# A two-block network in fp32: the mixer's products without halves, GpSimd freed in the first layer, and streamed buffers on multiples of 256

## The reference

```
h = rmsnorm(x) * (1 + scale) + shift          # channel by channel
layer 0:  u = h @ w_in                        # 1024 x 1024
          per group g of 256 channels, window w in (2, 4, 8, 16):
            pooled = trailing mean of u over w positions - u
            y_g = pooled @ w_grp[g]           # 256 x 256
          y = (concat(y_g) * scale) @ w_out   # 1024 x 1024
layer 1:  y = dilated attention (three branches, 16 heads each) @ w_o
x = x + gate * y
x = x + gate2 * ((silu(conv3(a)) * v) @ w_down), [a, v] = h @ w_up   # 2816 wide
```

## Time and profile before

| | |
|---|---|
| median of 3 runs | 2838.7 us (2837.08 to 2839.62) |
| the profiled execution | 2840.38 us, span 2838.6 us |
| TensorE busy | 2723.9 us, 96% of the span |
| VectorE busy | 1523.9 us, 54% |
| ScalarE busy | 1062.1 us, 37% |
| GpSimd busy | 388.6 us, 14%, nearly all in the first fifth |
| moved by DMA | 297.19 MB, 105 GB/s on average |
| chain that ended last | 89% TensorE, 3% VectorE, 1% ScalarE |

### The profile page before, as it was taken

How to read it: one execution, slowest core, us unless ns; L and a number is a source line. 1 busy time by engine, 2 the same in 40 slices (tenths; PEclk the granted TensorE clock), 3 DMA queues, 4 the chain that set the end, 5 groups by cost and what they waited for, 6 DMA issues and landing times.

```text
span 2838.6 us, 30758 instructions
## 1 busy us (share of the span) xinstructions
PE 2723.9 (96%) x12742; PEld 2186.1 (77%) x12742; DVE 1523.9 (54%) x2035; ACT 1062.1 (37%) x1488; POOL 388.6 (14%) x196
## 2 busy tenths in 40 slices
PE   5689999989999999899999999999999999999998
PEld 3568888778888887688888777788887777788886
DVE  7888857655555555654345555443344455443343
ACT  3333233344444444343234455422223455422231
POOL 3444545410000000000000001010010011010010
PEclk9799999999999999999999999999999999999999
DMA  7354645321212111122222221222223212223222
GB/s 271 119 210 183 248 177 198 135 83 60 75 61 74 69 66 60 60 89 101 95 89 102 97 75 60 76 102 97 89 95 113 90 60 75 76 103 101 85 100 71
DMA packets 45690, 297.19 MB, mean 105 GB/s; under 512 B 4976, under 2 KB 5104, under 8 KB 16368
## 3 DMA queue, kind: packets, MB, share of 16 engines
q1 hardware_dynamic: 45408, 294.71, 28.6%
q10 hardware_dynamic: 144, 0.52, 0.1%
HBM read 293.12 MB, written 2.10 MB: 104 GB/s over the span
## 4 chain that ended last, share of the span: by engine, by line
PE 89%; DVE 3%; ACT 1%; issue 1%; POOL 0%; DVEq 0%; ACTq 0%; POOLq 0%
PE PS L433 87%; PE PS L478 2%; DVE XT L1237 0%; DVE H2Lb L1234 0%; DVE WL L1234 0%; ACT H1H L821 0%; DVE AA L1234 0%; DVE H1L L1234 0%; DVE AR L1256 0%; ACT WH L821 0%; DVE T0c L1234 0%; DVE T1a L1234 0%; DVE T1c L1234 0%; ACT AA L821 0%; DVE T0a L1234 0%
## 5 line engine op out<-in xcount | busy, mean ns | idle before, releaser
L433 PE MATMUL PS<-H1H,WH 128*128 128x512 f32 x2240 | 898.2, 401 | 39.0 <-DVE H1L L1234 32.5
L433 PE MATMUL PS<-H1H,WL 128*128 128x512 f32 x2240 | 878.6, 392 | 0.0
L433 PE MATMUL PS<-H1L,WH 128*128 128x512 f32 x2240 | 877.8, 392 | 0.0
L1234 DVE TENSOR_TENSOR WL<-RAW,WH 128x1024 fp32r<-128x1024 f32 (+1 forms) x330 | 435.2, 1320 | 381.4 <-ACT WH L821 380.5
L821 ACT ACTIVATE WH<-RAW 128x1024 fp32r<-128x1024 f32 (+2 forms) x409 | 449.9, 1102 | 268.5 <-PE PS L433 257.7
L433 PEld LDWEIGHTS PS<-H1H,WH 128*128 128x128 f32 x2240 | 424.2, 189 | 143.6 <-issue 44.7
L433 PEld LDWEIGHTS PS<-H1L,WH 128*128 128x128 f32 x2240 | 424.8, 190 | 90.5 <-issue 5.3
L433 PEld LDWEIGHTS PS<-H1H,WL 128*128 128x128 f32 x2240 | 423.9, 189 | 91.0
L1687 POOL TENSOR_TENSOR WL<-RAW,WH 128x1024 fp32r<-128x1024 f32 (+2 forms) x79 | 229.8, 2914 | 235.8 <-ACT WH L821 235.6
L1256 DVE CUSTOM_DVE_ANT_0 AR<-AR,COND,CO 128x1024 f32<-128x1024 f32 x112 | 237.3, 2161 | 0.4
L433 PE MATMUL PS<-H2Hb,WH 128*128 128x512 f32 x384 | 160.0, 417 | 11.5 <-DVE H2Lb L1234 11.5
(11 more groups left out here) (246 smaller groups left out, 3334.3 us busy)
## 6 DMA issues: line engine op xcount, KB each, us to landing
RAW<-stream SPq DMA_DIRECT2D x170, 1024.0 KB, 4.8
AR<-stream SPq DMA_DIRECT2D x56, 1024.0 KB, 6.9
RAW<-stream SPq DMA_DIRECT2D x64, 704.0 KB, 4.0
RT<-ret SPq DMA_DIRECT2D x2, 1536.0 KB, 6.3
RAW<-stream SPq DMA_DIRECT2D x4, 640.0 KB, 6.9
XT<-xt SPq DMA_DIRECT2D x2, 1024.0 KB, 8.9
y<-XT SPq DMA_DIRECT2D x8, 256.0 KB, 2.5
ATT<-att SPq DMA_DIRECT2D x1, 576.0 KB, 3.4
```

Of the source, the lines that this page charges most:

```text
L433: return nc.tensor.matmul(out, weights, moving, start=start, stop=stop, skip_group_check=True)
L1234: return nc.vector.tensor_tensor(out, a, b, op)
```

## The change

- **Mixer without halves.** The input products (64 of them: 8 output chunks by 8 blocks) and the group products (16) are single fp32 matmuls on the raw weights and on an unsplit activation: HF takes the place of H1H and H1L for the input, PM that of H2Ha and H2La. ScalarE and GpSimd no longer make halves of tiles 0 to 8 or of the pooled chunks; VectorE writes the pooled chunk straight to PM. The first four weight units get buffers of their own (MIX0 to MIX3, over WH and WL).
- **Groups one by one.** The group products run group by group, both output halves in turn, and `w_out` takes its input chunks in the order in which they are made.
- **GpSimd idle ahead of the attention.** VectorE makes all low halves of weights from tile 9 on and all low halves in the norms.
- **Modulation.** The gates are computed between the last input chunks and behind the group products, the other units of the mixer between out products by explicit calls; AR has five slots for the first 16 units, then three. SP issues six units ahead of the small table `BAS`, in place of four.
- **Addresses.** Every streamed activation and weight buffer starts on a multiple of 256 bytes; the others are moved to make room.

```diff
-        units += [shift[i], scale[i], ("main", None, [("pool_w_in", 0, 2 * i, 2, 8 - GRP, GRP)])]
-    side = ada("ada_w", 0, 16, list(range(16, 48)))
+        units += [scale[i], shift[i], ("mix", None, [("pool_w_in", 0, 2 * i, 2, 8 - GRP, GRP)])]
+    gate = ada("ada_w", 0, 16, list(range(16, 24)))
...
-    units += pool[:1]
-    out, side = mix(pool[1:], side, 2)
+    units += pool[:1] + gate[:2] + pool[1:2] + gate[2:]
+    out, side = mix(pool[2:], ada("ada_w", 0, 24, list(range(24, 40))), 2)
...
-BYDVE = 79
+SLOTS = [n % 5 if n < 16 else n % 3 for n in range(sum(1 for u in UNITS if u[0] == "ada"))]
+SPLIT = 9
...
-        self.H1H, self.H1L = at("H1H", 17536, 4096, F32R), at("H1L", 33920, 4096, F32R)
+        self.H1H, self.H1L = at("H1H", 18432, 4096, F32R), at("H1L", 35072, 4096, F32R)
-        self.WH = [at(f"WH{i}", 66688 + 5632 * i, WSLOT, F32R) for i in range(3)]
-        self.WL = [at(f"WL{i}", 83584 + 5632 * i, WSLOT, F32R) for i in range(3)]
+        self.WH = [at(f"WH{i}", 68096 + 5632 * i, WSLOT, F32R) for i in range(3)]
+        self.WL = [at(f"WL{i}", 84992 + 5632 * i, WSLOT, F32R) for i in range(3)]
+        self.MIX = [at(f"MIX{i}", a, 1280) for i, a in enumerate((68096, 73728, 79360, 84992))]
+        self.PM, self.HF = at("PM", 159744, 4096), at("HF", 18432, 4096)
-        self.AH, self.AL = at("H2Hb", 109632, 4096, F32R), at("H2Lb", 126016, 4096, F32R)
+        self.AH, self.AL = at("H2Hb", 110592, 4096, F32R), at("H2Lb", 127488, 4096, F32R)
-        self.GH = [at("GHa", 158784, 5632, F32R), at("GHb", 130112, 5632, F32R)]
-        self.GL = [at("GLa", 181312, 5632, F32R), at("GLb", 152640, 5632, F32R)]
+        self.GH = [at("GHa", 160768, 5632, F32R), at("GHb", 131328, 5632, F32R)]
+        self.GL = [at("GLa", 183808, 5632, F32R), at("GLb", 153856, 5632, F32R)]
-        gh, gl = at("GHd", 113728, 5632, F32R), at("GLd", 136256, 5632, F32R)
+        gh, gl = at("GHd", 114688, 5632, F32R), at("GLd", 139264, 5632, F32R)
-        self.HH, self.HL = at("H2Hc", 113728, 4096, F32R), at("H2Lc", 130112, 4096, F32R)
+        self.HH, self.HL = at("H2Hc", 115456, 4096, F32R), at("H2Lc", 132096, 4096, F32R)
...
+    def plain(t, H, ready, freed):
+
+        b = BANK[t]
+        w, sem, value = c.whole(t)
+        q.wait_ge(sem, value)
+        vacate(b)
+        for k in range(8):
+            q.wait_ge(*ready(k))
+            ins = mm(PS[b][:, :], w[:, 128 * k:128 * k + 128], chunk(H, k), k == 0, k == 7)
+        ins.then_inc(c.mm, 1)
+        free[b] = freed
...
-                ins = three(x, t, 128 * (GRP * j + x), chunk(c.H1H, k), chunk(c.H1L, k), k == 0, k == 7)
+                o = 128 * (GRP * j + x)
+                ins = mm(PS[x][:, :], w[:, o:o + 128], chunk(c.HF, k), k == 0, k == 7)
...
-    for d in range(2):
-        t = 7 + d
-        q.wait_ge(*c.low(t))
-        for e, g in enumerate(GROUPS):
+    for e, g in enumerate(GROUPS):
+        for d in range(2):
...
-                q.wait_ge(c.pl, POOLED.index(n) + 1)
-                ins = three(b, t, 128 * n, chunk(c.PH, n), chunk(c.PL, n), i == 0, i == 1)
+                q.wait_ge(c.p3, POOLED.index(n) + 1)
+                ins = mm(PS[b][:, :], w[:, 128 * n:128 * n + 128], chunk(c.PM, n), i == 0, i == 1)
...
+    for i in range(8):
+        pooled(i)
+    prep(9)
+    for e, g in enumerate(GROUPS):
+        for d in range(2):
             n = 2 * g + d
...
+    prep(10)
+    modulation()
+    modulation()
     for n in range(8):
         prep(11 + n)
+        q.wait_ge(c.ada, 12)
         residual(RES["pool"], n, 9 + n, 16)
         add_square(1, n)
+        modulation()
```

More of the change, by code:

```diff
@@ L285, in __init__ @@
[L285 to L294, removed]
@@ L389, in low, with whole, slot @@
     def low(self, t):
-        return (self.lop, t + 1) if t < BYDVE else (self.lod, t + 1 - BYDVE)
+        return self.lod, t + 1 - SPLIT
+    def whole(self, t):
+        u, j = TILES[t]
+        n = PLACE[u]
+        if UNITS[u][0] == "mix":
+            return self.MIX[n], self.mix[n], 16
+        o = sum(words(x) for x in UNITS[u][2][:j])
+        return self.RAW[n % 2][:, o:o + words(UNITS[u][2][j])], self.raw[n % 2], 16 * (n // 2 + 1)
+    def slot(self, u):
+        n = PLACE[u]
+        i = SLOTS[n]
+        return self.AR[i], self.ara[i], 16 * SLOTS[:n + 1].count(i)
     def narrow(self, u, hh):
@@ L513, in pe_program @@
     for n in range(3):
-        gemm(4 + n, c.H1H, c.H1L, h, (c.pu, POOLED.index(n) + 1))
-    for d in range(2):
-        t = 7 + d
-        q.wait_ge(*c.low(t))
-        for e, g in enumerate(GROUPS):
+        plain(4 + n, c.HF, mixed_in, (c.pu, POOLED.index(n) + 1))
+    for e, g in enumerate(GROUPS):
+        for d in range(2):
             b = BANK["grp", d, g]
+            w, sem, value = c.whole(7 + d)
+            q.wait_ge(sem, value)
             vacate(b)
@@ L884, in act_program @@
         high(0, 0, 2 * i + 1, 0, 0)
-    prep(5)
-    def pooled(i):
-        n = POOLED[i]
+    for i, n in enumerate(POOLED):
         b = n - 3 if i < 5 else BANK[4 + n]
@@ L1230, in dve_program @@
     PS = c.PS
-    made, unit, adas, steps = 0, 0, 0, 0
+    made, adas, steps = SPLIT, 0, 0
+    ada = [u for u in range(len(UNITS)) if UNITS[u][0] == "ada"]
     def tt(out, a, b, op):
@@ L1244, in step, with modulation @@
         q.wait_ge(c.vstep, steps)
-    def modulation(u):
+    def modulation():
         nonlocal adas
-        AR, first = c.AR[adas % 3], UNITS[u][1]
-        q.wait_ge(c.ara[adas % 3], 16 * (adas // 3 + 1))
+        first = UNITS[ada[adas]][1]
+        AR, sem, value = c.slot(ada[adas])
+        q.wait_ge(sem, value)
         q.wait_ge(c.cond, 1)
@@ L1770, in load @@
     def load(u):
-        n, dst = PLACE[u], None
-        if UNITS[u][0] == "ada":
-            dst, sem = c.AR[n % 3], c.ara[n % 3]
-            q.wait_ge(c.ada, n - 2)
-        else:
+        n = PLACE[u]
+        if UNITS[u][0] == "mix":
+            dst, sem = c.MIX[n], c.mix[n]
+        elif UNITS[u][0] == "main":
             dst, sem = c.RAW[n % 2], c.raw[n % 2]
             if n >= 2:
-                before = [t for t, (v, _) in enumerate(TILES) if PLACE[v] == n - 2][-1]
-                q.wait_ge(*c.low(before))
+                before = [t for t, (v, _) in enumerate(TILES) if UNITS[v][0] == "main" and PLACE[v] == n - 2][-1]
+                q.wait_ge(*(c.low(before) if before >= SPLIT else (c.mm, mm_at(before))))
+        else:
+            dst, sem, _ = c.slot(u)
+            earlier = [m for m in range(n) if SLOTS[m] == SLOTS[n]]
+            if earlier:
+                q.wait_ge(c.ada, earlier[-1] + 1)
         src = c.stream[UOFF[u]:UOFF[u + 1]].rearrange("(p n) -> p n", p=128)
@@ L1790, in sp_program @@
     after = {TILES[t][0]: t for t in (ATT0 + 5, IN0 + 5, IN1 + 5)}
-    for u in range(4, len(UNITS)):
+    for u in range(6, len(UNITS)):
         load(u)
```

261 lines of the change are left out of this document (105 added, 156 removed).

## The result

| | before, timed beside it | after |
|---|---|---|
| median | 2839.16 us (2837.08 to 2840.28, 4 runs) | 2795.53 us (2793.53 to 2796.37, 4 runs) |
| profiled execution, span | 2840.38, 2838.6 | 2793.53, 2791.5 |

The ratio is 0.9846, 95% interval 0.9829 to 0.9863: 43.6 us or 1.5% faster. The forecast was 2684. The direction was right and the time lies inside the range, but the size was far off: 111 us of the expected gain are missing, and the time is nearest to rival B (2785).

What follows compares the result with a forecast made beforehand. TensorE was taken to bound the kernel, with some 66 us idle in the mixer and the stream's rate elsewhere. 2840.4 - 29.5 (mixer) - 126 (addresses) - 1.7 (profiled run above median) = 2683, told as 2684; range 2652 to 2815.

Steps and rivals of the forecast that it cites:

- rival B: Streamed products: a step of 128 bytes counts, H1 stays at 226.7 ns, buffers 64 past gain 24 us; 2785, chance 0.27.
- Part 1: Product stream outside the mixer's input: starts on multiples of 256 bring 216.1 ns an instruction, 126 us gained.
- The argument from the full fp32 product: Full fp32 streams at half the rate and leaves 2.8 ns an instruction that the operand supply can't explain.
- A: Streamed products: the excess vanishes on a multiple of 256; 2684 at 216.1 ns, 2656 at 213.3, chance 0.48.
- C: Streamed products: addresses do nothing, something else in these stages differs; 2809, chance 0.10.
- the slow level: TensorE's 1.2 GHz level: 426 ns an instruction, 512/1.2, no excess, so operand supply keeps up there.
- the supply of 8 bytes a cycle: Operand supply at 1.2 GHz: excess is the distance to the next multiple of 256, 13.3 or 20 ns.
- Part 2: Mixer's input products: 64 fp32 products at 0.859 us replace triples, running from 21.8 to 78.7 us.
- Part 3: Mixer's pooling and group products: last pooling 81.8, sixteen products without gap to 92.4, out products 31 to 35 us earlier.
- Part 4: Mixer's out products: VectorE's 54 us of work and 12 of waits; FFN scaling at 154.1, not 183.57, 29.5 us gained.
- Part 5: First FFN: VectorE takes over idle GpSimd's work, 9.2 us per two tiles under TensorE's 10.88; cost nothing.

Runs made afterwards that it cites:

- e2: The kernel before with only its streamed buffers moved to the changed kernel's offsets, the rest moved to make room: 2819.41 us, ratio 0.9930.
- e1: No network, only stretches of 48 products with varied starts of moving operand and weights: 226.7 ns at equal position modulo 256, 229 at 64, 232 to 234 otherwise.
- e3: The changed kernel with H1H (and HF in its place) 64 bytes further and H1L 64 lower: 2816.38 us, ratio 0.9919.
- e5: The changed kernel with only the weight buffers (WH, WL, MIX) 128 bytes lower, no moving operand touched: 2847.39 us, ratio 1.0027.
- e9: No network, only stretches of 48 products with varied widths, weight columns, rows, banks and offsets: 226.6 ns at 128 weight columns, 230.0 at 64, 231.7 at 32.
- e8: The changed kernel with GpSimd given 24 subtractions in the mixer whose results nobody reads: 2801.81 us, ratio 0.9868.
- e4: The kernel before with VectorE making the low halves of weights from tile 17 on, GpSimd only the mixer's: 2839.20 us, ratio 0.9998.
- e6: The changed kernel with four more modulation loads spread over five buffers instead of three: 2789.19 us, ratio 0.9824.
- e7: As e6, with three more modulation units moved into VectorE's idle time before the pooling and their loads moved ahead: 2780.49 us, ratio 0.9793.

## Why the prediction was right or wrong

**Part 1, the addresses: wrong, and it is the failed step.** It was "I take 213.3 + 2.8 = 216.1 ns" for a start on a multiple. The spacing is 226.7 at best. So H1's 6528 instructions gained nothing (69 us foreseen) and the others 6.6 ns instead of 17.2: 24 us in all where 126 were put, and 19.7 as e2 measures it. The two rates at hand (226.7 at 128 past, 233.3 at 64 past) were explained by the moving operand's distance to the next multiple of 256; this fits both points, but the weights lay 128 past in the same rows, and the difference to them fits as well (0 and -64). e1, e3 and e5 show that only the difference counts, and that 226.7 is its floor. The argument from the full fp32 product, that a slower supply removes the excess, held for full fp32 (429 ns a record again in e9) and didn't carry over: an fp32r product at equal position keeps 13 to 14 ns over its columns at 256, 320, 384 and 512 of them, also when it is given the same weights as the one before (their load is in the trace all the same). It says little about fp32r, since e3 and e5 show full fp32 at the same rate for distances of 0, 64 and 128. Rival B held this case in one half sentence, "if only their relative position counts the outcome is the same", and had 0.27 against A's 0.48; e2 alone (19.7 us for the addresses, B's 24) would have settled it between the two. Why an fp32r product keeps its 13 ns, and why the position adds to them, stays open. The range held the result because it was drawn wide enough for B and C, not because A's mechanism had any part in it.

The forecast's terms, held against the runs: 213.3 ns for 512 columns is what e9's widths give (0.417 ns a column), and the slow level's 426.7, read as no excess, is twice that, as at the start of e1. No run shows the 216.1 ns for fp32r: bfloat16 comes near it, with 215.8 in e1 and e9, fp32r keeps 226.7 at its best. Nor does any run show the supply of 8 bytes a cycle, which was an estimate from the two spacings: by its formula an operand 224 bytes past a multiple should take 216.7 ns, and in e1 (MK) it took 233.1.

**Part 2, the input products: right.** Pairs every 6.35 to 6.5 us (T at 20.23, 26.58, 33.12, 39.62), 0.859 us a product, first product 21.98 for 21.8, end 78.68 for 78.7. That GpSimd was what stretched the passes is shown by e8, which brings the stretching back, and by e4, which takes it away in the FFN; and every pass of the changed kernel lies between 1274 and 1286 ns.

**Part 3, pooling and group products: right.** The last pooled chunk, 81.8 foreseen, came at 82.0, the sixteen products ran from 78.68 without a gap, the output products from 92.0 for 92.5.

**Part 4, the output products: right in kind, its terms too small.** 12 us were put on waits. From 82 us to the scaling VectorE is busy 57.5 us (12 modulation units and 11 low halves of weights, where 11 and 9 were counted) and idle 23.2. The recorded terms, 54 us of work and 12 of waits from 82 us on, add up to 148 and not to 154.1; the other 6 us have no name in the prediction, and they hid a part of both errors. What was missed is SyncE's order: the last weight load sat behind modulation loads that waited for a buffer (part 4 named it, and priced it too low). e6 removes this and lands on the forecast's 154.1, which is in part luck, with 56.3 us of work and 16.0 idle. e7 shows that VectorE's work is next in line.

**Part 5, GpSimd in the first FFN: right.** e4: no difference (by the interval -3 to +2 us), TensorE 180.00 of 180 us in both, and in the changed kernel too.

**The sum.** 102 us missing from part 1, 8.6 from part 4: 2684 + 111 = 2795, against 2795.5. B's price was 2785, ten under, for part 4's reason.

## What to carry to other kernels

Before giving an effect of addresses a formula, list both operands' addresses: two points that differ in the moving operand may as well differ in its position against the weights. Put fp32r moving operands and weights at the same offset modulo 256 (226.7 ns a product of 512 columns here, against 229 to 234), and don't expect more from a rounder address. When a row says that TensorE waited for VectorE, look whether VectorE itself was idle, and follow the row back to the load and to what stood ahead of it in the queue; then move that work into an idle stretch that the timeline shows (8.7 us here).

## What the runs showed of the hardware that was not expected

- fp32r products of 512 columns with 128 weight columns: 226.7 ns with moving operand and weights at the same address modulo 256, 229 with the moving operand 64 bytes after the weights, 231.6 at 16 bytes, 232 to 234 at the other differences tried; in the slow start of e1, at equal position, 426.7, which is twice the columns' 213.3 with no excess.
- The floor is 13 to 14 ns over the columns at 512, 384, 320 and 256 columns (226.7, 174.0, 146.7, 119.8), but 16 at 448; 192 and 128 columns both take 111 to 112 ns, so there the columns no longer set the spacing. bfloat16 has 2.5 ns over its columns (215.8 at 512, 109.2 at 256), and a full fp32 record of 512 columns 429.1 ns, 2.4 over twice its columns, whether the moving operand lies 0, 64 or, taken modulo 256, 128 bytes from the weights.
- Fewer weight columns make it slower, not faster: 230.0 ns at 64, 231.7 at 32, with moving operand and weights at the same position.
- 512-column subtractions on GpSimd and modulation passes on VectorE alternated whole in e8, in rounds of 2.21 us, where lone passes follow each other every 1.21.
